# Moving a sample batch's row transposes and key waits on the tensor queue of a hybrid attention step

## What is computed

```python
s = einsum(q, k) * scale + bias         # NSA selected and window, compressed, MoBA, memory heads
p = masked_softmax(s)                   # NSA ones times their gates
o_nsa = g0 * (p_cmp @ v_cmp) + g1 * (p_sel @ v_sel) + g2 * (p_win @ v_win)
o_moba = p_moba @ v_moba
o_mem  = p_mem @ v_mem
x + sum(sigmoid(g_b) * ((o_b * silu(z_b)) @ w_b) for the three branches b) @ w_out
```

## Time and profile before

| | |
|---|---|
| time, median of 3 runs | 1119.33 us (1119.31 to 1120.62) |
| profiled execution | 1120.33 us, its span 1118.5 us |
| busy: TensorE products / weight loads | 1105.0 / 1082.0 us |
| busy: VectorE, ScalarE, GpSimd | 617.9, 421.7, 66.0 us |
| moved by DMA | 202.04 MB, 181 GB/s in the mean |
| chain that ended last | 92% TensorE, 4% VectorE, 2% DMA |

### The profile page before, as it was taken

How to read it: one execution, slowest core, us unless ns; L and a number is a source line. 1 busy time by engine, 2 the same in 40 slices (tenths; PEclk the granted TensorE clock), 3 DMA queues, 4 the chain that set the end, 5 groups by cost and what they waited for, 6 DMA issues and landing times.

```text
span 1118.5 us, 19507 instructions
## 1 busy us (share of the span) xinstructions
PE 1105.0 (99%) x8064; PEld 1082.0 (97%) x8064; DVE 617.9 (55%) x906; ACT 421.7 (38%) x574; POOL 66.0 (6%) x111
## 2 busy tenths in 40 slices
PE   8999999999999999999999999999999999999996
PEld 7998999999999999999999999999999999999996
DVE  6974443536446767675555557454454454454445
ACT  6633322424335444453333334333333333333332
POOL 0014000000000000000101000000000000002220
PEclk9999999999999999999999999999999999999998
DMA  8546775544445233349797844444444444464442
GB/s 295 187 169 195 249 262 193 183 152 146 172 140 185 81 114 113 112 151 307 262 308 266 269 142 169 167 168 163 171 166 164 169 150 148 152 244 146 150 150 94
DMA packets 64097, 202.04 MB, mean 181 GB/s; under 512 B 6598, under 2 KB 35814, under 8 KB 45718
## 3 DMA queue, kind: packets, MB, share of 16 engines
q1 hardware_dynamic: 59048, 186.63, 48.6%
q0 software_dynamic: 2400, 10.89, 2.9%
q10 hardware_dynamic: 2574, 3.46, 0.9%
HBM read 193.61 MB, written 11.53 MB: 183 GB/s over the span
## 4 chain that ended last, share of the span: by engine, by line
PE 92%; DVE 4%; DMA 2%; ACT 1%; issue 1%; SPq 1%; DVEq 0%; ACTq 0%
PE bank L1272 26%; PE bank L1273 26%; PE bank L1274 26%; DMA raw<-in_stream 2%; DVE w_lo L764 1%; PE bank L1604 1%; PE bank L1377 1%; PE bank L1372 1%; PE bank L1351 1%; PE bank L1350 1%; PE bank L1349 1%; PE bank L1500 1%; DVE m_lo L791 1%; ACT w_hi L499 1%; PE bank L1439 0%
## 5 line engine op out<-in xcount | busy, mean ns | idle before, releaser
L499 ACT ACTIVATE w_hi<-raw 128x2048 fp32r<-128x2048 f32 x141 | 270.1, 1915 | 574.3 <-PE bank L1274 530.0
L1272 PE MATMUL bank<-h_hi,w_hi 128*128 128x320 f32 x1552 | 484.9, 312 | 0.8 <-DVE w_lo L764 0.8
L1274 PE MATMUL bank<-h_hi,w_lo 128*128 128x320 f32 x1552 | 479.6, 309 | 0.0
L1273 PE MATMUL bank<-h_lo,w_hi 128*128 128x320 f32 x1552 | 479.5, 309 | 0.0
L764 DVE TENSOR_TENSOR w_lo<-raw,w_hi 128x2048 fp32r<-128x2048 f32 x141 | 327.6, 2324 | 180.2 <-ACT w_hi L499 180.1
L1272 PEld LDWEIGHTS bank<-h_hi,w_hi 128*128 128x128 f32 x1552 | 291.4, 188 | 5.6 <-issue 3.9
L1273 PEld LDWEIGHTS bank<-h_lo,w_hi 128*128 128x128 f32 x1552 | 291.5, 188 | 0.4
L1274 PEld LDWEIGHTS bank<-h_hi,w_lo 128*128 128x128 f32 x1552 | 291.3, 188 | 0.0
L1273 PE MATMUL bank<-oz_lo,w_hi 128*128 128x320 f32 x256 | 78.9, 308 | 0.0
L1274 PE MATMUL bank<-oz_hi,w_lo 128*128 128x320 f32 x256 | 78.8, 308 | 0.0
L1272 PE MATMUL bank<-oz_hi,w_hi 128*128 128x320 f32 x256 | 78.8, 308 | 0.0
(11 more groups left out here) (341 smaller groups left out, 1122.1 us busy)
## 6 DMA issues: line engine op xcount, KB each, us to landing
raw<-in_stream SPq DMA_DIRECT2D x141, 1024.0 KB, 4.9
cmp_t<-in_cmp_pages SPq DMA_DIRECT2D x32, 128.0 KB, 4.2
kt_moba<-in_moba_k SPq DMA_DIRECT2D x16, 256.0 KB, 4.7
kt_mem<-in_mem_k SPq DMA_DIRECT2D x8, 512.0 KB, 6.1
vs_moba<-in_moba_v SPq DMA_DIRECT2D x16, 256.0 KB
vs_mem<-in_mem_v SPq DMA_DIRECT2D x8, 512.0 KB
out_win_old<-in_cache_win POOLq DMA_DIRECT2D x8, 512.0 KB, 4.2
raw<-in_stream SPq DMA_DIRECT2D x11, 256.0 KB, 8.8
```

Of the source, the lines that this page charges most:

```text
L499: nc.scalar.activation(w_hi[:, u], raw[:, u], ACT.Copy).then_inc(hi_ready[u], 1)
L1272: nc.tensor.matmul(out[:, 0:n], w_hi[:, u, kb, :], hi[:, kb, :], start=(kb == first), stop=False)
L1273: nc.tensor.matmul(out[:, 0:n], w_hi[:, u, kb, :], lo[:, kb, :], start=False, stop=False)
L1274: mm = nc.tensor.matmul(out[:, 0:n], w_lo[:, u, kb, :], hi[:, kb, :], start=False, stop=(kb == last))
```

## The change

- On TensorE, `sample_columns(b - 1)` comes directly behind `sample_turn(b)`, one batch later than before. Only the last batch keeps its place between the halves of `part(1)`; the others' `part(1)` is in one piece.
- The two waits at the head of `sample_scores(b + 1)` are a function of their own, `sample_staged`, which is called ahead of `sample_values(b)`.
- ScalarE's two copies and VectorE's addition of batch `b - 1` move to trip `b`: on ScalarE ahead of `gate0_tile(0, b)`, on VectorE behind the three copies of transposed probabilities. The last batch's stay where they were.

SP's and GpSimd's lists are the same as before.

```diff
--- before.py
+++ after.py
@@ -695,14 +695,20 @@
                 act.wait_ge(w_free[u], b + (J_G0 + 2))
                 nc.scalar.activation(g0_t[:, b * 2 + u, :], g0_t[:, b * 2 + u, :], ACT.Tanh, scale=0.5).then_inc(g0_rdy, 1)
 
-            for b in range(DEC_BATCH):
-                gate0_tile(0, b)
-                if b + 1 < DEC_BATCH:
-                    sample_exps(b + 1)
+            def columns_out(b):
                 act.wait_ge(bo_ready, b + 1)
                 nc.scalar.activation(o_win[:], OB[:, 64:P], ACT.Copy).then_inc(bo_copied, 1)
                 nc.scalar.activation(o_t[:, NSA_H:HEADS, SEQ + b * DEC_SEQ:SEQ + (b + 1) * DEC_SEQ],
                                      OB[:, P:3 * P].rearrange("p (h t) -> p h t", t=32)[:, :, 0:DEC_SEQ], ACT.Copy).then_inc(bo_copied, 1)
+
+            for b in range(DEC_BATCH):
+                if b:
+                    columns_out(b - 1)
+                gate0_tile(0, b)
+                if b + 1 < DEC_BATCH:
+                    sample_exps(b + 1)
+                if b + 1 == DEC_BATCH:
+                    columns_out(b)
                 gate0_tile(1, b)
 
             def oz_high(h0, h1):
@@ -1102,6 +1108,13 @@
                 dve.wait_ge(mm_done[u], b + (J_G0 + 2))
                 nc.vector.tensor_tensor(g0_t[:, b * 2 + u, :], W[u][:, 0:TOK], inv[:], ALU.mult).then_inc(w_free[u], 1)
 
+            def columns_added(b):
+                dve.wait_ge(bo_ready, b + 1)
+                dve.wait_ge(bo_copied, 3 * b + 2)
+                nc.vector.tensor_tensor(o_t[:, 0:NSA_H, SEQ + b * DEC_SEQ:SEQ + (b + 1) * DEC_SEQ],
+                                        OB[:, 0:64].rearrange("p (h t) -> p h t", t=DEC_SEQ),
+                                        o_win[:].rearrange("p (h t) -> p h t", t=DEC_SEQ), ALU.add).then_inc(bo_copied, 1)
+
             dve.wait_ge(z_done, HEADS)
             for b in range(DEC_BATCH):
                 dve.wait_ge(bpt_ready, b * 3 + 1)
@@ -1110,17 +1123,16 @@
                 nc.vector.tensor_copy(ptb[1][:].rearrange("p n c -> p (n c)"), P1[:, 0:384]).then_inc(bpt_copied, 1)
                 dve.wait_ge(bpt_ready, b * 3 + 3)
                 nc.vector.tensor_copy(ptb_mem[:].rearrange("p n c -> p (n c)"), S2[:, 0:256]).then_inc(bpt_copied, 1)
+                if b:
+                    columns_added(b - 1)
                 gate0_scaled(0, b)
                 dve.wait_ge(brow_ready, b + 1)
                 nc.vector.tensor_copy(o_rows[:].rearrange("p n c -> p (n c)"), OB[:, 0:384]).then_inc(brow_copied, 1)
                 split_lo(0, b + (J_G0 + 1))
                 if b + 1 < DEC_BATCH:
                     sample_softmax(b + 1)
-                dve.wait_ge(bo_ready, b + 1)
-                dve.wait_ge(bo_copied, 3 * b + 2)
-                nc.vector.tensor_tensor(o_t[:, 0:NSA_H, SEQ + b * DEC_SEQ:SEQ + (b + 1) * DEC_SEQ],
-                                        OB[:, 0:64].rearrange("p (h t) -> p h t", t=DEC_SEQ),
-                                        o_win[:].rearrange("p (h t) -> p h t", t=DEC_SEQ), ALU.add).then_inc(bo_copied, 1)
+                if b + 1 == DEC_BATCH:
+                    columns_added(b)
                 gate0_scaled(1, b)
                 split_lo(1, b + (J_G0 + 1))
 
@@ -1475,9 +1487,11 @@
                                               start=(kb == 0), stop=(kb == 1))
                 mm.then_inc(o_ready, 1)
 
-            def sample_scores(b):
+            def sample_staged(b):
                 pe.wait_ge(b_staged, b * 3 + 3)
                 pe.wait_ge(kt_in, b * 96 + 96)
+
+            def sample_scores(b):
                 for g in range(GROUPS):
                     nc.tensor.matmul(S0[32 * g:32 * g + 32, 272:272 + N_CMP], q_smp[:, b, REP * g:REP * g + REP, :].rearrange("p h t -> p (h t)"),
                                      kc[:, b * 2 + g, :], start=True, stop=True)
@@ -1558,20 +1572,27 @@
                     prompt_scores(i + 1)
                 else:
                     pe.wait_ge(bias_in, 32)
+                    sample_staged(0)
                     sample_scores(0)
                 part(1, i + J_Z, h_hi, h_lo, TOK, ALL)
             for b in range(DEC_BATCH):
                 part(0, b + J_G0, h_hi, h_lo, TOK, PART_A)
                 sample_turn(b)
+                if b:
+                    sample_columns(b - 1)
                 part(0, b + J_G0, h_hi, h_lo, TOK, PART_B)
                 part(0, b + J_G0, h_hi, h_lo, TOK, PART_C)
+                if b + 1 < DEC_BATCH:
+                    sample_staged(b + 1)
                 sample_values(b)
                 if b + 1 < DEC_BATCH:
                     sample_scores(b + 1)
-                part(1, b + J_G0, h_hi, h_lo, TOK, PART_A)
-                sample_columns(b)
-                part(1, b + J_G0, h_hi, h_lo, TOK, PART_B)
-                part(1, b + J_G0, h_hi, h_lo, TOK, PART_C)
+                    part(1, b + J_G0, h_hi, h_lo, TOK, ALL)
+                else:
+                    part(1, b + J_G0, h_hi, h_lo, TOK, PART_A)
+                    sample_columns(b)
+                    part(1, b + J_G0, h_hi, h_lo, TOK, PART_B)
+                    part(1, b + J_G0, h_hi, h_lo, TOK, PART_C)
 
             for k in range(KB // 2):
                 for br in range(2):
```

## The result

| | before | after |
|---|---|---|
| time, median (range) | 1120.62 us (1119.31 to 1121.23), 5 runs | 1126.82 us (1126.26 to 1128.11), 6 runs |
| ratio of the two, 95% interval | | 1.0059 [1.0049, 1.0069] |
| profiled execution, its span | 1120.33 us, 1118.5 us | 1127.32 us, 1125.5 us |
| from batch 0's first score product to batch 7's first value product | 148.09 us | 153.39 us |
| behind it, to the end of the span | 472.2 us | 472.2 us |

A sixth run of the kernel before took 1470.11 us, 350 us more than the other five, and is left out. The kernel is slower by 6.2 us by the medians and by 6.6 us by the ratio (5.5 to 7.7 by its interval). The forecast was 1128.2 us: 8.9 us more than 1119.33, the median of the three runs of the kernel before that were known then. So the sign and the range held and the size was too large.

A forecast was written before the change was run, and what follows sets the result against it. TensorE, busy for 99% of the span, was taken to bound the kernel. Key lateness 7.48 us plus restarts 1.4 us gave 8.9 us, on the 1119.33 us median: 1128.2 us, range 1123.0 to 1131.4 us.

The forecast's parts named there:

- Moving the transposes costs 0: TensorE's row transposes: 0.110 us each wherever they stand, so 0, with a bound of -0.1 to 0 us.
- The keys' wait is the term that matters: Ahead of the values on TensorE: waiting there for the next batch's keys exposes their late landing, 8.9 us with restarts.
- Lateness, 7.48 us: Next batch's keys land 0.19 to 1.85 us after the values' normal start, seven times, 7.48 us in all.
- Restart, 0.2 us each: TensorE's delay from the keys' landing to the values' start: 0.2 us, seven times 1.4; bounds 0.1 and 0.35.
- Stalls don't pay for each other: Across batches: a stall moves values, next key issue and next landing alike, so the lateness comes back in each batch.
- The weights' term of 1 us, left at 0: Second-half weight transfer goes out earlier behind the keys; sharing engines might delay landings, some 1 us, kept for the upper end.
- The gaps of today are not gained: TensorE's gaps ahead of the scores, 0.32 us: not saved, since the time from values' end to next landing isn't shortened.
- Rival A: DMA load eases as stalls lengthen batches, keys land 0.19 us late after the first: 4.4 us, 1123.7 us; chance 0.20.
- B: Rival: keys come 1.66 us late in each of the six later loads: 13.2 us, 1132.5 us; chance 0.10.
- C: Rival: keys land early enough that their wait costs nothing: 1119.0, or 1121.1 us with batch 0's stall; chance 0.08, shared.
- D: Rival: merging the transposes saves 0.6 us more, 1118.4 us with the gaps gone; chance 0.08, shared with the no-cost rival.
- The clock: TensorE's granted clock in the sample stage: forecast wrong if it leaves 1.00 in the stalls; no size given.

The follow-up runs named there:

- with the staging wait: Kernel after with the keys' wait put back ahead of the scores, leaving transposes, copies and GpSimd staging wait moved: 1120.65 us, 1.0000 of before.
- the small keys: Kernel after with the keys of batches 1 to 7 read for only 16 of 128 partitions: 1120.20 us, 0.9996 of before.
- more bytes: Kernel after with seven 512 KB window-cache copies issued by SP right ahead of the keys: 1136.56 us; same copies in the kernel before: 1123.32 us.
- keys first: Kernel after with SP issuing the next keys ahead of the first half's weight tile: 1123.99 us; same swap in the kernel before: 1120.16 us.
- weights behind keys: Kernel after with SP holding the second half's weight tile until the next batch's keys have landed: 1124.94 us, 1.0036 of before.

## Why the prediction was right, and where it was off

- **What bounds the kernel** held: TensorE, and nothing behind the stage gave anything back (472.2 us in every profile, to within 0.05).
- **Moving the transposes costs 0** held, to the digit: 0.110 us each, eleven in a row, and no time when moved alone. The copies behind them were never late: the values are entered in 0.24 us in every batch of that kernel.
- **The staging wait costs 0** held, by the run with that wait alone.
- **The keys' wait is the term that matters** held: put in alone it costs what the change costs, and it costs nothing once the keys land earlier. The idle time is where it was forecast, behind the landing of the next batch's keys, in batches 0 to 6 and not in 7 (in the second execution of the change not in batch 5 either, whose keys land in time).
- **Lateness, 7.48 us** was mis-sized, and it is the larger part of the over-forecast. It was read well from its rows, but from one execution; three others with the keys' wait in its old place give 4.5, 8.3 and 3.8, a mean of 6.0 with the first. Landings measured from the values' end are 17.0 to 17.8 us in the mean of six loads in every kernel with this SP order and these bytes, and single ones 16.5 to 18.7. In before's first profile the last of a load's 96 completions came 1.3 us behind the last but one in three of seven loads, those of batches 1, 3 and 5, whose 1.85, 1.66 and 1.21 us made up 4.7 of the 7.48. Why it was late in these isn't known.
- **Restart, 0.2 us each** was mis-sized: the values start 0.09 us behind the landing in each stalled batch, and where the wait is met nothing is lost at all. Seven times 0.09 are 0.6 us, not 1.4. With both corrected, and less the 0.50 us that came back at the scores, the sum is 6.0 + 0.6 - 0.5 = 6.1 us. Measured were 5.3 and 5.9 in the stage in two executions, and 6.2 by the medians and 6.6 by the ratio over the whole. With lateness between 3.8 and 8.3 from one execution to the next, a closer match would mean nothing.
- **The starting point** was luck. The forecast of the time stood on 1119.33 us, the median of three runs; the five runs have 1120.62. So the size was 2.7 us too large (8.9 against 6.2) and the time only 1.4 (1128.2 against 1126.82).
- **Stalls don't pay for each other** held: with the wait in batch 0 only, the cost is that of one stall.
- **The weights' term of 1 us, left at 0.** Held back behind the keys the weight tile gave no earlier landing as a whole (17.30 us against 17.36 and 17.34). Two small effects of opposite sign can't be told apart in it.
- **The gaps of today are not gained** was slightly off: 0.50 us came back at the scores (above). I had argued that keys come a fixed time behind the values' end. They do, but with the wait ahead of the values the scores never wait again, so the gaps go and their time is in the stall.
- **Rival A** (the load eases) isn't borne out: six loads land 17.75, 17.26, 17.76 and 17.05 us behind the values' end in the four executions whose values don't stall (before twice, the transposes alone, with the staging wait), and 17.36, 17.34 and 17.05 in three whose values do (after twice, the waits alone). The means, 17.46 and 17.25, differ by less than executions of one kind do; the change's time of 1126.8 lies between A's 1123.7 and the forecast, but not for A's reason. **B** fell: it had 1.86 us of idle time in each batch behind batch 0, and the two profiles of the change show at most 1.41, the mean being 0.7. **C**'s mechanism is real and was shown with the small keys, no cost at all, but the keys of the kernel are too late for it. **D** fell with the transposes alone: 0.9998 could hide its 0.6 us, but the eleven in a row take 1.50 us in after's profile, what 0.110 each gives, and in the profile of the transposes alone the batches behind the first take 18.72 to 18.73 us, as before.
- **The clock** was named as unpriced, and it is a term missing from the sum. With a stall of the length that I forecast for batch 0, 2.05 us, it fell in one profiled execution, at a cost of 1.67 us. In neither profile of the change did it fall in the stage. Half of after's six runs show the lower mean clock, so my estimate is that it may be worth up to about 0.8 us (half of 1.67) in the mean; that isn't shown. The over-forecast terms covered it.

## What to carry to other kernels

A wait that is moved up a queue brings into the open the part of its event's lateness that the work between its old place and its new one used to cover. So ask of each wait what work that is: it is the cover that goes. Where a cost is a sum of small differences between a transfer's landing and an engine's arrival, read it from at least two executions before its size is trusted: here the same code gave 7.5 and 4.5 us, and near relatives of it 8.3 and 3.8. And don't price a stall of some 2 us at its length alone: it may take the clock along.

## What I had not expected of the hardware

- TensorE's granted clock fell to 1.2 GHz for 3.4 us after idle stretches of 1.97 us (batch 0 only), 2.29 and 2.35 us (more bytes) and 2.39 us (start of after). It stayed at 2.4 GHz after idle stretches of 1.84 us (keys first) and 1.95 us (weights behind keys). These are six places in five kernels and no more; at which length it falls can't be read from them. The Trainium skill, TensorE: Matmul & The Clock Gate, Part 1, says that a TensorE left idle goes back to half the clock and gets the full one back by being busy; the two levels in these rows, 0.50 and 1.00, agree.
- A load of six transfers is as late as its last completion, which in three of seven loads of one execution came 1.3 us behind the last but one of 96; in before's second execution it was at most 0.8.
- A queue of transfers is paced by its issuing too: SP takes 9.65 us from the first to the last of fourteen of them (keys first), and taking a weight tile out of their way moved the last issue by 0.5 us in the mean (11.1 to 10.6 us behind the values' end).
